# A two-block transformer kernel: modulation weights in single pieces between dense slabs, another turn order in both attentions, and padded operand addresses

## What is computed

```python
u = h @ w_in                                  # 1024 x 6484
ys = [mamba2(...), fox_attn(...), moba_attn(...), dsa_attn(...)]   # 8 heads of 64 each
merged = sum(sigmoid(h @ w_gate + b_gate) * (ys @ w_branch))
x = x + rms_norm(merged @ w_out); x = x + rms_norm(swiglu(rms_norm(x)))
```

```python
sh1, sc1, g1, sh2, sc2, g2 = split(silu(c) @ w_mod + b_mod, 6)     # w_mod: 1024 x 6144 per layer
p = (rms_norm(x) * (1 + sc1) + sh1) @ w_in                          # 1024 x 2560
o = differential attention, 4 heads, softmax(m=0) - lam * softmax(m=1), 256 rows x 512 keys
x = x + g1 * (concat(gmlp(p), rms(o), conv31(p)) @ w_out)
h = rms_norm(x) * (1 + sc2) + sh2
x = x + g2 * ((silu(dwconv3(h @ w_gate)) * (h @ w_val)) @ w_down)   # 1024 -> 2816 -> 1024
```

## Time and profile before

| | |
|---|---|
| median of three runs | 2511.81 us (2507.24 to 2511.85) |
| the profiled execution, its own time | 2500.43 us |
| its span | 2498.8 us |
| busy TensorE matmul / weight load | 2247.9 us (90%) / 1796.6 us (72%) |
| busy VectorE / ScalarE / GpSimd | 1425.2 us (57%) / 1044.5 us (42%) / 303.8 us (12%) |
| mean DMA rate | 140 GB/s |

### The profile page before, as it was taken

How to read it: one execution, slowest core, us unless ns; L and a number is a source line. 1 busy time by engine, 2 the same in 40 slices (tenths; PEclk the granted TensorE clock), 3 DMA queues, 4 the chain that set the end, 5 groups by cost and what they waited for, 6 DMA issues and landing times. The chain is left out here.

```text
span 2498.8 us, 29164 instructions
## 1 busy us (share of the span) xinstructions
PE 2247.9 (90%) x11116; PEld 1796.6 (72%) x11116; DVE 1425.2 (57%) x2187; ACT 1044.5 (42%) x1664; POOL 303.8 (12%) x310
## 2 busy tenths in 40 slices
PE   8999898898999998979997877889989898887999
PEld 6777676787777776768876664667767787656997
DVE  5665574454465647545445886554444325966774
ACT  4545554443444455534443434322222223543443
POOL 0017120000000532210000540000000000600000
PEclk9999999999999999989998988889999998987999
DMA  7644335565555433466564213423333435333554
GB/s 227 185 124 127 105 115 160 181 177 183 191 175 157 141 102 95 138 201 180 160 205 159 63 51 93 135 93 110 101 101 110 135 101 168 94 119 117 162 183 161
DMA packets 184121, 349.15 MB, mean 140 GB/s; under 512 B 11824, under 2 KB 23216, under 8 KB 183984
## 3 DMA queue, kind: packets, MB, share of 16 engines
q1 hardware_dynamic: 183984, 347.29, 44.4%
HBM read 346.19 MB, written 1.05 MB: 139 GB/s over the span
## 5 line engine op out<-in xcount | busy, mean ns | idle before, releaser
L816 DVE TENSOR_TENSOR wlo<-wraw,whi 128x1024 fp32r<-128x1024 f32 (+1 forms) x538 | 646.2, 1207 | 682.0 <-ACT whi L1009 678.7
L1009 ACT ACTIVATE whi<-wraw 128x1024 fp32r<-128x1024 f32 (+1 forms) x552 | 562.7, 1027 | 648.0 <-PE psum L1770 546.3
L1770 PE MATMUL psum<-whi,act_h 128*128 128x512 f32 (+2 forms) x1424 | 578.4, 406 | 31.8 <-DVE p L1320 22.1
L1770 PE MATMUL psum<-wlo,act_h 128*128 128x512 f32 (+2 forms) x1424 | 564.7, 397 | 0.0
L1770 PE MATMUL psum<-whi,act_l 128*128 128x512 f32 (+2 forms) x1424 | 563.8, 396 | 0.0
L1770 PEld LDWEIGHTS psum<-whi,act_h 128*128 128x128 f32 x1424 | 277.1, 195 | 105.6 <-DVE p L1320 24.7
L1770 PEld LDWEIGHTS psum<-whi,act_l 128*128 128x128 f32 x1424 | 275.7, 194 | 62.2
L1770 PEld LDWEIGHTS psum<-wlo,act_h 128*128 128x128 f32 x1424 | 276.6, 194 | 56.5
L1770 PE MATMUL psum<-act_h,whi 128*128 128x512 f32 (+1 forms) x704 | 244.0, 347 | 23.7 <-DVE wlo L816 19.8
L1770 PE MATMUL psum<-act_l,whi 128*128 128x512 f32 (+1 forms) x704 | 242.2, 344 | 0.0
L1770 PE MATMUL psum<-act_h,wlo 128*128 128x512 f32 (+1 forms) x704 | 242.2, 344 | 0.0
(11 more groups left out here) (270 smaller groups left out, 2693.4 us busy)
## 6 DMA issues: line engine op xcount, KB each, us to landing
wraw<-in_w_in SPq DMA_DIRECT2D x136, 512.0 KB, 3.7
wraw<-in_w_gate SPq DMA_DIRECT2D x104, 512.0 KB, 3.7
wraw<-in_w_mod SPq DMA_DIRECT2D x96, 512.0 KB, 3.7
wraw<-in_w_ffn_in SPq DMA_DIRECT2D x80, 512.0 KB, 3.7
wraw<-in_w_ffn_out SPq DMA_DIRECT2D x44, 512.0 KB, 4.2
wraw<-in_w_down SPq DMA_DIRECT2D x44, 512.0 KB, 4.3
wraw<-in_w_val SPq DMA_DIRECT2D x40, 512.0 KB, 4.6
wraw<-in_w_branch SPq DMA_DIRECT2D x32, 512.0 KB, 3.9
```

The lines of the kernel that those rows point to most:

```text
L816: eng.tensor_tensor(wlo[:, i, 0:st.n, 0:st.w], wraw[:, st.s % RING_W, 0:st.n, 0:st.w], whi[:, i, 0:st.n, 0:st.w].bitcast(F32), ALU.subtrac ...
L1009: nc.scalar.activation(whi[:, d % RING_S, 0:st.n, 0:st.w], wraw[:, s % RING_W, 0:st.n, 0:st.w], ACT.Copy).then_inc(sem("slab_rounded"), 1)
L1770: return nc.tensor.matmul(out, lhsT, rhs, start=start, stop=stop)
```

## The change

1. Modulation weights are laid out on the host's side as 48 pieces for each layer, of all 1024 rows by 128 columns, 4 KB in a row for each partition (`w_mod_pieces`). A piece is one slab of the ring: 8 matmuls of 128 columns, two rounds over the four strips.
2. The pieces of shifts and scales (32 for each layer, 64 in all) ride in the first block: one behind the first slab of every group of four in every dense product on two tiles, from slab 12 on, and its reader two slabs later. No chunk stands at the stage changes any more.
3. The 8 pieces of the first gate stand in the second block's attention, the 8 of the second gate ride in the feed-forward, one every fifth slab with a reader two slabs later. Bank 7 is kept for them.
4. The exponentials become steps of their own. First block: scores i, values i-3, turning i-2, exponentials i. Second block: scores i, values i-3, turning i-2, exponentials i, mix i-1.
5. ScalarE takes all of the `w_in_2` results out of PSUM.
6. Pads put `act_h`, `act_l`, `y_h`, `y_l`, `hid_h`, `hid_l`, `act2_h`, `act2_l`, `hid2_h` and `hid2_l` all at 384 modulo 512; `whi` and `wlo` stay at 128.
7. The silu of c moves to an early step of the first layer.

```diff
+OPERAND_AT, OPERAND_STEP = 384, 512
@@ gemm
+            if pl.mod_every:
+                pl.mod_since += 1
+                if pl.mod_queue and pl.mod_since % pl.mod_every == 0:
+                    st.after = mod_ride(pl, pl.mod_bank)
+                elif pl.mod_since % pl.mod_every == pl.mod_gap:
+                    st.after = mod_reader(pl, pl.mod_bank)
+            elif (pl.mod_queue or pl.mod_last) and tiles == 2 and st.s >= 3 * RING_W:
+                at, slabs_in = k // SLAB_K, -(-nk // SLAB_K)
+                if pl.mod_queue and at % 4 == 0 and at + 3 < slabs_in:
+                    st.after = mod_ride(pl, pl.next_bank())
+                elif at % 4 == 2:
+                    st.after = mod_reader(pl, pl.next_bank())
+def mod_ride(pl, bank):
+    l, c = pl.mod_queue.pop(0)
+    n = len(pl.mod_reads) + len(pl.mod_last)
+    st = Step(kind="slab", s=len(pl.slabs), weight="w_mod_2", layer=l, c=c, evac="mod", mc=n, banks=[pl.bank(bank)],
+              first=True, last=True, war=pl.mod_reads[n - 2] if n >= 2 else [])
...
+def mod_reader(pl, bank):
+    if not pl.mod_last:
+        return []
+    st = pl.mod_last.pop(0)
...
@@ plan_first
-                for kind, h in (("attn_s", i), ("attn_v", i - 3), ("attn_t", i - 2)):
+                for kind, h in (("attn_s", i), ("attn_v", i - 3), ("attn_t", i - 2), ("attn_e", i)):
-        mods = mod_slabs(pl, 0, filler.pop(0))
-        pl.steps += mods + waiting + mod_reader(pl, mods, pl.misc)
+        pl.steps += waiting
@@ plan_second
-        for i in range(len(units) + 2):
-            for kind, u in (("att2_m", i - 1), ("att2_t", i - 2), ("att2_s", i), ("att2_v", i - 2)):
+        for i in range(len(units) + 3):
+            for kind, u in (("att2_s", i), ("att2_v", i - 3), ("att2_t", i - 2), ("att2_e", i), ("att2_m", i - 1)):
+        pl.mod_queue, pl.mod_every, pl.mod_since = [(l, c) for c in MOD_GATES[1]], 5, 0
-        pl.turns = tuple(range(8))
+        pl.turns = tuple(range(7))
@@ SBUF
+        def at_offset(name, stack):
+            n = (OPERAND_AT - nc.sbuf_base) % OPERAND_STEP
+            if n:
+                sb(name, [P, n // 4], F32, stack)
+        at_offset("pad_common", ctx)
+        at_offset("pad_one", one)
-        rstd4 = sb("rstd4", [P, 4], F32, two)
         with ExitStack() as own:
             hid2_h = sb("hid2_h", [P, KF, 4 * P], F32R, own)
...
         p = sb("p", [P, 4, IN_COLS], F32, two)
+        rstd4 = sb("rstd4", [P, 4], F32, two)
@@ ScalarE, VectorE
                     if st.evac == "p":
-                        for t in range(0, st.tiles, 2):
+                        for t in range(st.tiles):
-                    if st.evac == "p":
-                        for t in range(1, st.tiles, 2):
-                            filled(dve, st.banks[t])
-                            dve.tensor_copy(p[:, t, st.col:st.col + st.w], psum[:, st.banks[t][0], 0:st.w]
-                                            ).then_inc(free(st.banks[t]), 1)
-                if st.kind == "attn_s":
+                if st.kind == "attn_e":
@@ TensorE
-                    for k in range(st.n):
-                        for i in range(2):
-                            r = 32 * (2 * k + i)
-                            ins = dot(psum[r:r + 32, bk[0], 0:half], condm[:, st.kt + k, :],
-                                      wraw[:, st.s % RING_W, k, i * half:(i + 1) * half], st.first, st.last)
+                    for k in range(KD):
+                        r = 32 * (k % 4)
+                        ins = dot(psum[r:r + 32, bk[0], 0:P], condm[:, k, :], w[:, k * P:(k + 1) * P], k < 4, k >= 4)
```

More of the change, by code:

```diff
@@ L102, in misc @@
     def misc(self):
[L104 removed]
+        return self.bank(self.free[self.tick("free_turn") % len(self.free)])
     def gemm_bank(self):
@@ new lines, in gemm @@
+    return steps
+MOD_COLS = list(range(0, 2 * KD)) + list(range(3 * KD, 5 * KD))
+MOD_GATES = (list(range(2 * KD, 3 * KD)), list(range(5 * KD, 6 * KD)))
+def mod_ride(pl, bank):
[3 more added lines that the diff above has]
+              first=True, last=True, war=pl.mod_reads[n - 2] if n >= 2 else [])
+    b, use = st.banks[0]
+    st.used = (f"psum_full{b}", use + 1)
+    pl.slabs.append(st)
+    pl.mod_last.append(st)
+    return [st]
@@ new lines, in mod_reader @@
+def mod_reader(pl, bank):
+    if not pl.mod_last:
+        return []
+    st = pl.mod_last.pop(0)
+    l, c, part = st.layer, st.c, st.c // KD
+    bk = pl.bank(bank)
+    pl.mod_reads.append([(f"psum_full{bk[0]}", bk[1] + 1)])
+    if part in (2, 5):
+        return [Step(kind="mod_gate", l=l, c=c, mc=st.mc, gate=part // 3, j=c % KD, waits=drained(*st.banks), banks=[bk])]
+    steps = [Step(kind="mod_cols", l=l, c=c, mc=st.mc, waits=drained(*st.banks), banks=[bk])]
+    if part in (1, 4) and c % KD == KD - 1:
+        steps.append(Step(kind="mod_gain", l=l, i=part // 3, waits=drained(bk)))
@@ L209, in mod_reader @@
     return steps
 def plan_first(pl):
-    filler = list(MOD_COLS)
+    pl.mod_queue = [(i, c) for i in range(DEPTH) for c in MOD_COLS]
     for l in range(DEPTH):
@@ L393, in plan_first @@
             hidden += waiting
-        mods = mod_slabs(pl, 0, filler.pop(0))
-        pl.steps += mods + waiting + mod_reader(pl, mods, pl.misc)
+        pl.steps += waiting
         out = gemm(pl, "w_ffn_out", l, "hid", 2, KF, 0, D, "mix", ready=split_ready(hidden))
         pl.steps += out
[L398 to L404, removed]
+        postnorm(2 * l + 1, out)
 def plan_second(pl):
-    filler = [(0, MOD_COLS[-1])] + [(1, c) for c in MOD_COLS]
+    assert not pl.mod_queue and not pl.mod_last
+    pl.mod_bank, pl.mod_gap, pl.turns = 7, 2, (0, 1, 2, 3)
     for l in range(DEPTH):
@@ L566, in plan_second @@
             pl.tick("hid_lo", w // P)
-            if late:
-                pl.steps += mod_reader(pl, late, pl.misc)
-            late = fill() if c in (0, 1, 2, 3) else None
-            pl.steps += late or []
-        late = fill()
-        pl.steps += late
-        if late:
-            pl.steps += mod_reader(pl, late, pl.misc)
+        assert not pl.mod_queue and not pl.mod_last
+        pl.mod_every = 0
         pl.turns = (0, 1, 2, 3)
@@ L591, in build @@
         plan_second(pl)
+    pl.steps = [one for st in pl.steps for one in [st] + st.after]
     slabs, dense = pl.slabs, pl.dense
@@ L641, in build @@
         cossin2 = sb("cossin2", [P, 2, 2, 2, 16])
-        stream = sb("stream", [P, 4])
+        stream = sb("stream", [P, 2])
         cond = sb("cond", [P, KD, 2])
         condm = sb("condm", [P, KD, 32])
-        modrow = sb("modrow", [P, 2, NW // 2])
+        modrow = sb("modrow", [P, 2, P])
         sums4 = sb("sums4", [P, 4, 2])
@@ L1832, in _ @@
                     fill(pe, st.banks[0])
[L1833 to L1836 removed]
+                    dot(psum[:, st.banks[0][0], 0:2], modrow[:, st.mc % 2, :], stream[:, :]).then_inc(full(st.banks[0]), 1)
                 if st.kind == "mod_gate":
                     need(pe, st.waits)
[L1840 to L1845 removed]
+                    bk = st.banks[0]
+                    fill(pe, bk)
+                    for i in range(2):
+                        ins = dot(psum[:, bk[0], i * P:(i + 1) * P], stream[:, i:i + 1].to_broadcast([P, P]),
+                                  modrow[:, st.mc % 2, :])
+                    ins.then_inc(full(bk), 1)
                 if st.kind in ("modsplit", "ysplit"):
@@ L2041, in constants @@
     cs2 = np.stack([np.cos(ang2), np.sin(ang2)], 1).reshape(2, P, 64).transpose(1, 0, 2).reshape(P, 128)
-    rows = np.zeros((P, 4))
-    for half in range(2):
-        for s in range(2):
-            rows[[32 * half + s, 64 + 32 * half + s], 2 * half + s] = 1
+    rows = np.zeros((P, 2))
+    for j in range(4):
+        rows[[32 * j, 32 * j + 1], [0, 1]] = 1
     return np.concatenate([eye, upto, np.ones((P, P)), later, zero, later, later.T, zero, later.T, cs, neg, cs2, rows],
```

129 lines of the change are left out of this document (52 added, 77 removed).

## The result

The changed kernel took 2441.03 us. The ratio to the kernel before is 0.9717, 95% interval 0.9695 to 0.974. That is 71 us less where 135 were forecast. 2441.03 lies 1 us above the range, which no run here can tell from its edge; that half of the gain is missing is far outside the noise. The profiled execution took 2444.05 us, with a span of 2442.4.

The account below looks back on a forecast made before the run. The prediction took TensorE as the bound, busy 2247.9 of 2498.8 us. Its terms summed to -135 us from the profiled 2500.4, so 2365, or 2377 us as the median of runs; range 2325 to 2440.

Parts of the forecast that it names:

- Does a ride stall the ring?: Pieces in the weight ring: next slab ready after 6.2 us, TensorE comes after 9.3, so no loss put down.
- the term of the rides: First block: 64 pieces with readers at 0.9 us each on TensorE, +58 us, bounds 48 to 83.
- the ring stalls: Rival: late slabs stop TensorE at each of 80 pieces in dense stages; 2577 us at 2.5 each; chance 0.06.
- Stage changes of the first block: Removing fillers there saves 8.2, 5.9 and 10.2 us in each of two layers, 5 at the first layer's end.
- Second feed-forward: Second block: it had no filler and gets 8 riding pieces, +10 us.
- First feed-forward: Second block: 46 us of loss become 8 rides, 10 us, and 1.5 of cold start, -35 us.
- Second-block attentions with what follows the first: New order and half the gate work leaving, -13 and -16 us; filler gone behind the first attention, -8.
- First-block order: First block's attentions: ScalarE copies `probT` before waiting for the maximum, -12 us, bounds 0 to -22.
- The clock: First block: two thirds of about 12 us lost at half clock behind seven fillers goes, 8 us.
- Pads: Dense 512-column matmuls: rate follows operand start, -34 us, bounds 0 and -42; rival without effect 2411, chance 0.15.
- `w_in_2`: VectorE drops 17 copies of 0.684 us, about 12 before the split ending the stage: -8 us, +3 to -14.
- Norms: Second block: two modulated norms lose their chunk, -10 us.

Follow-up runs that it names:

- no_rides: The changed kernel without the first block's 64 pieces of shifts and scales and their readers, so that computation is left out: 0.9351 of the kernel before, 2349 us.
- no_strips: The changed kernel with each piece computed on all 128 output columns, 8 matmuls into one sum, none side by side: 1.0017 of the kernel before, 2516 us.
- pads_off: The changed kernel without the pads, operands starting where they did before (0, 352 and 384 modulo 512): 0.98 of the kernel before.
- before_pads: The kernel before with the pads alone added: 0.9888 of the kernel before, 28 us less.
- p_split_back: The changed kernel with every second `w_in_2` result moved out of PSUM by VectorE again: 0.9734 of the kernel before.

## Why the prediction was off

**The step that failed** is "Does a ride stall the ring?", with its "3.1 us of slack, and I put nothing down", and with it the term of the rides, 58 us. They cost 92. The pieces' own price was right or even high (1.01 us for 0.9 where bare, 0.77 to 0.86 over the whole block once the waits are gone); the 37 to 48 us that the two edits give back in the first block are waits that stood in no term. The slack was worked out for one piece among full slabs and an idle VectorE. Behind the piece at 604.26, among slabs of 256 columns, the same sum leaves none: TensorE comes after a reader and three slabs, 0.3 + 3 x 1.4 = 4.5 us, but the slab needs 4.85 + 1.06 + 1.23 = 7.1. SyncE has to wait for TensorE's use of the piece, so the lead of the transfers over ScalarE is gone (11 waits became 87). At the narrow slabs of 256 and 340 columns, which I had passed over with "1 to 3 us in all", and where VectorE's list is full, TensorE stands 2 to 7 us, and behind the longest of these stands it comes back at half clock. The rival "the ring stalls" named this, but as a loss at every piece or none; it happens at some. In the first block a buffer of their own for the pieces gives back 16 us by the ratios and 25 by the traces, in the second feed-forward 12.

**A wait that the prediction didn't have** is the reader's. I counted its 0.21 us on TensorE, and one sentence allowed 0.4 for banks, but I didn't ask what VectorE has ahead of the read and who needs the bank next. Moving the reader by one slab is worth 21 to 24 us.

The bare price, ring and reader come to 65 + 16 + 21 = 102 us for the first block, against 92 measured (by the traces 65 + 25 + 21 = 111 against 97). The bare price is too much for the sum, as 49 to 55 us are left when the other two are gone.

The other terms, forecast and found:

- Stage changes of the first block, -54: the seven took 84 us before and 41 after, -43. Most of the missing 11 us, 8.5, stand at the two changes from `w_ffn_in` to `w_ffn_out`, 7.4 and 2.5 us where I left 0.7. Without any piece (no_rides) these two still take 3.1 and 3.8, and all seven 40.6.
- Second feed-forward, +10: +23. The ring is 12 of it and the pads are 3.
- First feed-forward, -35: it and the filler behind it took 303.7 us and take 252.2, of which the pads are 7: -44.
- Second-block attentions with what follows the first, -37: the stages are 20.3 and 12.7 us shorter, -33; 16 of it is the order, the rest the gate pieces and the filler that left. First-block order, -12: -22 by the ratios, -11 by the trace, so about as forecast; but the wait for `probT`, at 12.8 us, stayed above the 8 that I had named.
- The clock, -8: its gain can't be told from the new cold stretches. The first block's granted clock is 0.96 for 0.97, so none came in sum.
- Pads, -34: the rate follows the start, as said, but -28 alone and -21 in the changed kernel (-22 and -10 by the traces). One to 3 us of the difference are the 256-column product, which I put at nothing; another part is the slow return to the stride behind the strips (below). The rest is open.
- `w_in_2`, -8: -2 to -3. Norms, -10: -2.

The sum of the pads' 13 us, the ring and reader's 34, the second feed-forward's 13, the stage changes' 11, the attentions' 4, and 13 for `w_in_2` and the norms is 88; 19 came back in the first feed-forward and the first block's order. That leaves 69 for the 64 us by which the forecast missed. It is no proof of the shares: the pads' 3 us in the second feed-forward stand in two terms, and with the trace's 11 us for the first block's order 10 fewer came back.

## What to carry to other kernels

A buffer that one engine frees late makes the whole ring late. Here it helped to give the guest with another life time a buffer of its own and to let the look-ahead count only the slabs that it serves; that a plain fifth buffer would have done less is not shown. When small work is put between dense work, its price on the busy engine is the easy part: follow also its result, to the engine that must read it, to what stands ahead in that engine's list, and to the next user of the bank. Slack is to be worked out for the shortest slab and the fullest list, not for the mean.

## What the runs showed of the hardware

- **The stride recovers slowly behind the strips.** Medians over all bare pieces of the changed kernel: the intervals of the dense matmuls behind a piece are 341, 240, 235, 233, 236, 224, 231, 236, 228, 232, 231 ns, and then 227. That is 0.06 us more than at 227 from the second on. It isn't the interruption as such: behind a piece over all 128 columns (no_strips) they are 314, 233, 231, and then 227. In pads_off they swing between 229 and 238 from the second on, around the stride of 0.2337 that they have there anyway. So a little of the pads' gain is lost behind each piece in strips.
- **The best start depends on the width.** At 384 modulo 512 a 512-column matmul starts every 227 ns for 233 or 234, but a 256-column one every 120 for 117 (medians; the means of the 256-column ones are nearer, 119.8 for 118.3, and pads_off's feed-forward of them is 3 us shorter, before_pads's 1 us longer than that of the kernel before).
- **VectorE beside GpSimd.** The same operation of 256 elements takes 0.43 us before GpSimd's adds begin at 1466.80 and 1.37 while they run:

```profile
1462.85 0.43 DVE L1452 TENSOR_TENSOR p<-aT 128x256 f32<-128x256 f32 x1
...
1469.99 1.37 DVE L1452 TENSOR_TENSOR p<-aT 128x256 f32<-128x256 f32 x1
```

```profile
1466.80 8.48 POOL L974 TENSOR_TENSOR cacc<-cacc,ctmp 128x502 f32<-128x502 f32 x6
```

The Trainium skill (SBUF — State Buffer, Who interferes with whom) says that a VectorE instruction with two SBUF inputs and a GpSimd instruction that reads SBUF contend for a shared pair of ports, which is an exclusive lock. 1.37 us is 0.43 and most of one of GpSimd's adds (8.48 / 6 = 1.41), which agrees. It doesn't hold beside every GpSimd instruction: next to the power of 8 elements just before, VectorE's multiplication with two SBUF inputs took 0.69 us, as it does alone:

```profile
1464.34 2.49 POOL L927 TENSOR_TENSOR ssq<-ssq,minus_half 128x8 f32<-128x8 f32 x1
...
1465.25 0.69 DVE L1436 TENSOR_TENSOR p<-p,ssq 128x512 f32<-128x512 f32 x1
```

In the kernel before, the rotation was over at 1452.7, when GpSimd's adds began at 1452.84; in the changed one it falls under them, and TensorE's wait for the scaling of k is 16.5 us instead of 7.8. That isn't because VectorE was free of its copies of `p`: in p_split_back, which has them back, the same operation takes 1.34 us beside the adds, and TensorE waits 12.2 us for a copy of `p` instead. So the copies, moved or not, leave the stage about as long; what brought rotation and adds together is open.
